# Another order of three ScalarE steps at four layer boundaries, and 17 matmuls of constants in two gaps of TensorE

## The chip, the core and the metric

The kernel runs on one core of a Trainium2 chip. The time is the device time of one execution in microseconds (us); lower is better. Engines are named as in the profile: PE is TensorE (PEld its weight load), ACT is ScalarE, DVE is VectorE, POOL is GpSimd, SP is SyncE, which issues the DMAs.

## What is computed

Two blocks on a sequence of 512 tokens of width 1024, in float32. The first has a convolution layer and an attention layer, each followed by a feed-forward layer, the second a gated delta rule beside sliding-window attention, and another feed-forward layer. Cut to what matters here:

```python
for layer in range(2):
    hn = rms_norm(h, mix_pre_g[layer])
    m = conformer_conv(hn, ...) if layer == 0 else mla_attention(hn, ...)
    h = h + rms_norm(m, mix_post_g[layer])
    f = squared_relu_mlp(rms_norm(h, ffn_pre_g[layer]), w_ff1[layer], w_ff2[layer])
    h = h + rms_norm(f, ffn_post_g[layer])
```

So after each of the four layers stands the same sequence: square the layer's output, sum it over the width, take the root, scale, add to the residual `h`, normalise again, and multiply by the next layer's weights. This is a boundary.

## The kernel before

Everything is held with the width on the partitions: 8 tiles of 128 by 512 tokens. All weights come as one stream of chunks of 128 x 2048 (1 MB), two buffers deep. A float32 product is made of three products of a high and a low part. For each chunk ACT copies the high part (`head`, L626, `whi<-wraw`), then POOL (L535) or, for the chunks at a boundary, DVE (`weights_low`, L1279) subtracts it from the raw weights to get the low part (`wlo`), and then PE multiplies: 48 matmuls of 512 columns for a chunk (L2113), or at a boundary 48 of 256 columns for each half of the tokens (L2136, `project_half`). `start_chunk` makes PE wait for the semaphore `lo_ready` of the chunk before its first matmul.

The order on every engine is written out by hand, and each engine works through its own list in that order. The four boundaries are called MIX0, FFN0, MIX1 and FFN1 after the layer that they end; they are the same code with other numbers. At boundary `i`, `last` is the last chunk of the layer. In a boundary the tokens are done in two halves (0 and 1), and the tiles in four pairs (m = 0 to 3):

- PE: chunks `last-1` and `last`, both for half 0, then both for half 1; then `last+1` half 0, `last+2` half 0, `last+1` half 1, `last+2` half 1. In the middle of `last+1` half 0, ahead of its tile k = 4, PE sums the squares of the last pair of half 1 (`post_sums(i, 1, (3, 4))`, L2150).
- DVE: empties the banks (`evac`), scales by the root (L1293), adds to the residual (L1299), takes the low part of the next operand (`low`, L1304), and in between makes `weights_low(last+1)` and `weights_low(last+2)`. The second stands behind `low` of tiles 4 to 7 of half 0, ahead of everything of half 1.
- ACT: squares (`post_square`, L668), roots (L673, L674), the high part of the next operand (`high`, L679), and `head` of the chunks.

At FFN0 two operands are made from one residual (`xh`/`xl`, then `hh`/`hl`); the second's eight low parts of half 0 stand on DVE right behind `weights_low(last+2)`.

The other two places are in the first layer. At the start of the kernel PE sums the squares of x with a matrix of ones (L2204) and then multiplies the first chunk (L2113), as soon as DVE has made the low part of the first tile of the normalised x (L1259). While it runs, ACT makes the diagonal tap weights of the convolution (L764), copies the high part of chunk 2 (L626) and then takes the sigmoid (L769) of chunk 0's result; DVE gates with it (L1416), and PE multiplies the first taps (`taps`, L2227). Behind the convolution PE sums the convolution's output and its squares (L2249, L2254), ACT and DVE take mean, root and SiLU and split the result tile by tile into `hh` and `hl` (L1514), and PE multiplies chunk "pw2" (`project(c0, hh, hl, need=operand("ln"))`), each tile as soon as its `hl` is there.

Of the kernel before, what the change touches and what calls it, by code (L numbers as in the profile page):

```python
# [24 lines left out]
P = 128  # L25
# [3 lines left out]
DT = D // P  # L29
# [110 lines left out]
def build(nc, A, out):  # L140
    ctx = ExitStack()
    with ctx:
        def sb(name, shape, dt=F32):
            return ctx.enter_context(nc.sbuf_tensor(name, shape, dt))

        def sem(name):
            return ctx.enter_context(nc.semaphore(name))
# [15 lines left out]
        K = sb("K", [P, N_CONST])  # L163
        PV = sb("PV", [P, N_VEC])
        small = sb("small", [P, N_COLS])
        ps = ctx.enter_context(nc.psum_tensor("ps", [P, 8, SEQ], F32))
# [15 lines left out]
        ident, ones, half_ones = map(const, ("ident", "ones", "half_ones"))  # L182
# [12 lines left out]
        pool_sum, TAP_BANK, ODD_BANK = (E[:, 0, :], E[:, 1, :]), (6, 7), (4, 5)  # L195
# [115 lines left out]
        pair_free = [sem("pair_free_even"), sem("pair_free_odd")]  # L311
# [72 lines left out]
        def weights(c):  # L384

            if c < DT and c // 2 % 2:
                return lent[c % 2][:, 0:CW], lent[c % 2][:, CW:2 * CW]
            return whi[:, c % 2, :], wlo[:, c % 2, :]

        def weights_free(eng, c, h=0):  # L390

            if c >= DT + 2:
                eng.wait_ge(chunk_done, h * 2 + (c - 1))
            elif c >= 4:
                eng.wait_ge(chunk_done, c - 3)

        def pair(c):
            return 2 * (c % 2)
# [5 lines left out]
        def emptied(eng, c, h=0):  # L404

            eng.wait_ge(pair_free[c % 2], h + (c // 2 + 1))
# [202 lines left out]
        def _(act):  # L609
            steps = [0]  # L610

            def step(ins):

                steps[0] += 1
                ins.then_inc(act_step, 1)
                act.wait_ge(act_step, steps[0])

            def head(c, h=0):

                if isinstance(h, int) and c + 2 * h >= N_CHUNK:  # L620
                    return
                p = c % 2
                w = WIDTH[c + 2 * h] if isinstance(h, int) else CW
                act.wait_ge(raw_loaded[p], h * 16 + 16 * (c // 2 + 1))
                weights_free(act, c, h)
                act.activation(weights(c)[0][:, 0:w], wraw[:, p, 0:w], ACT.Copy).then_inc(hi_ready, 1)  # L626
# [32 lines left out]
            def boundary(i):  # L659
                last = LAST[i]  # L660

                def post_square(m, half):
                    if half:
                        emptied(act, last - 3 + m)
                    else:
                        act.wait_ge(evac_half, 2 * i + m - 1)
                    s = 2 * (m - 2)
                    act.activation(sq_half[:, s:s + 2, :], Y[:, 2 * m:2 * m + 2, TOK[half]],  # L668
                                   ACT.Square).then_inc(post_sq, 1)

                def post_root_of(half):
                    act.wait_ge(post_summed, 2 * i + half + 1)
                    step(act.activation(POST[half], POST[half], ACT.Ln, scale=1.0 / D, bias=eps_rms))  # L673
                    act.activation(POST[half], POST[half], ACT.Exp, scale=-0.5).then_inc(post_root, 1)  # L674

                def high(s, j, half):
                    (name, at, hi, _), hi_sem, _, _ = pre_norms(i)[s]
                    act.wait_ge(resid_half, DT * i + DT // 2 * half + j // 2 + 1)
                    act.activation(hi[:, j, TOK[half]], resid[:, j, TOK[half]], ACT.Copy,  # L679
                                   scale=vec(name, at + j)).then_inc(hi_sem, 1)  # L680

                def pre_squares(half):
                    for m in range(DT // 2):
                        act.wait_ge(resid_half, DT * i + DT // 2 * half + m + 1)
                        act.activation(Z[:, 2 * m:2 * m + 2, TOK[half]], resid[:, 2 * m:2 * m + 2, TOK[half]],
                                       ACT.Square).then_inc(pre_sq, 1)

                for m in range(2):
                    c = last - 3 + m
                    head(c + 2)  # L690
                    emptied(act, c)
                    if m:
                        act.wait_ge(post_added, 3 * i + 1)
                    for n in range(2):
                        act.activation(SQ[:, n, :], Y[:, 2 * m + n, :], ACT.Square).then_inc(post_sq, 1)
                    if m == 0 and i == MIX0:
                        act.wait_ge(rel_summed, 1)
                        act.activation(rel_rows, ps[0:SW_H, 6, 0:RELW], ACT.Copy).then_inc(rel_copied, 1)
                act.wait_ge(post_added, 3 * i + 2)
                post_square(2, 0)  # L700
                post_square(3, 0)
                post_root_of(0)
                head(last + 1)
                post_square(2, 1)
                for j in range(6):
                    high(0, j, 0)
                head(last + 2)
                post_square(3, 1)
                for j in range(6, DT):
                    high(0, j, 0)  # L710
                post_root_of(1)
                if i == FFN0:
                    for j in range(DT):
                        high(1, j, 0)
                pre_squares(0)
                for j in range(DT):
                    high(0, j, 1)
                if i == FFN0:
                    for j in range(DT):
                        high(1, j, 1)  # L720
                    head(last + 3)
                pre_squares(1)
# [34 lines left out]
            c0 = START["pw1"]  # L757
# [72 lines left out]
            c0 = START["pw2"]  # L830
# [39 lines left out]
            c0 = START["latent"]  # L870
# [233 lines left out]
            for t in range(TT):  # L1104
                par = t % 2
                act.wait_ge(rows_summed, t + 1)
                c0 = COLS["state_decay"][0] + 8 * par
# [962 lines left out]
        def _(pe):  # L2070
# [19 lines left out]
            def project(c, hi, lo, h=0, k_tiles=DT, k0=0, need=None, second=None, second_need=None,  # L2090
                        paired=True, midway=None, hooks={}, start=True, bank=None):

                if start:
                    start_chunk(c, h)
                p = c % 2
                bank = 2 * p if bank is None else bank

                order = ([(n, k) for k in range(k_tiles) for n in range(2)] if need and paired else
                         [(n, k) for n in range(2) for k in range(k_tiles)])
                for n, k in order:  # L2100
                    if midway and (n, k) == (1, 0):
                        midway()
                    if (n, k) in hooks:
                        hooks[(n, k)]()
                    if n and second:
                        hi, lo = second
                    if need and n == 0:
                        need(k)
                    if second_need and n == 1:
                        second_need(k)  # L2110
                    w = slice(k * 2 * P + n * P, k * 2 * P + (n + 1) * P)
                    for q, (wt, xt) in enumerate(passes(hi, lo, *weights(c))):
                        ins = pe.matmul(ps[:, bank + n, :], wt[:, w], xt[:, k0 + k, :],  # L2113
                                        start=k == 0 and q == 0, stop=k == k_tiles - 1 and q == 2)
                    if isinstance(h, int) and c == N_CHUNK - 1 and (n, k) == (0, k_tiles - 1):
                        ins.then_inc(last_half, 1)
                ins.then_inc(chunk_done, 1)
# [64 lines left out]
            def operand(name):  # L2182
                return lambda k: pe.wait_ge(split_done, SPLIT0[name] + k + 1)

            def project_tokens(c, k_tiles, n_out, need=None, hooks={}):
# [13 lines left out]
                                            start=k == 0 and q == 0, stop=k == k_tiles - 1 and q == 2)  # L2199
                ins.then_inc(chunk_done, 1)  # L2200

            pe.wait_ge(ones_loaded, 16)
            pe.wait_ge(squares_added, 1)
            pe.matmul(ps[:, SUMS, :], ones, Y[:, 0, :], start=True, stop=True).then_inc(squares_summed, DT)  # L2204
            c0 = START["pw1"]
            ready = operand("mix0_pre")

# [57 lines left out]
            rest_sum(DT - 1).then_inc(rest_summed, 1)  # L2265
            rest_square(DT - 1)
            c0 = START["pw2"]
            project(c0, hh, hl, need=operand("ln"))

            def distance_bias():  # L2270
# [9 lines left out]
            def ffn(layer):  # L2280
# [11 lines left out]
                with pe.Fori(1, FF_BLOCKS - 1) as b:  # L2292
# [12 lines left out]
                    bank=LATENT_BANK)  # L2305
# [281 lines left out]
            for t in range(TT):  # L2587
# [40 lines left out]
                for lv in range(1, 6):  # L2628
# [4 lines left out]
                    for g in range(2):  # L2633
                        pe.wait_ge(level_x, 10 * t + 2 * lv + g - 1)
                        for i in range(2):
# [3 lines left out]
                                            start=True, stop=True)  # L2639
# [11 lines left out]
                    for g in range(2):  # L2651
# [3 lines left out]
                        for i in range(2):  # L2655
                            hp = slice((2 * g + i) * P, (2 * g + i + 1) * P)
                            ip, up = slice(i * P, (i + 1) * P), slice(HALF + i * P, HALF + (i + 1) * P)
                            if lv < 5:
                                ins = pe.matmul(ps[:, LEVEL_Q[g], ip], inverse[g][:, up], level_mask[:, hp],  # L2659
                                                start=True, stop=True)  # L2660
                            else:
                                ins = pe.matmul(ps[:, LEVEL_Q[g], up], level_mask[:, hp], inverse[g][:, up],
                                                start=True, stop=True)
# [201 lines left out]
```

## Time and profile before

| what | value |
|---|---|
| time, median of 3 runs | 1952.64 us (1952.09 to 1953.35) |
| profiled execution: its time | 1951.87 us |
| its span, first to last instruction | 1950.1 us |
| PE busy, share of the span | 1909.4 us, 98% |
| DVE busy | 824.0 us, 42% |
| ACT busy | 783.3 us, 40% |
| POOL busy | 681.5 us, 35% |
| mean granted clock of PE | 0.999 |

Between the span and the profiled execution's time lie 1.8 us. PE is busy nearly always, but the busy time counts matmuls whose ends are modelled and overlap, so where PE really waits is read from its waits and from the distances between matmuls.

### The profile page before, as it was taken

To read this page: it belongs to the slowest core of one execution; us is meant where nothing else is said; L and a number is where in the kernel's file an instruction comes from. 1 tells how busy PE (TensorE), PEld (TensorE's weight loads), DVE (VectorE), ACT (ScalarE), POOL (GpSimd) and SP (SyncE) were. 2 spreads that over 40 slices of the span, in tenths; PEclk is the share of its full clock that TensorE was granted. 3 is DMA by queue.
4 is the path that set the end of the run, shared out by engine and by line. 5 is a ranking of instruction groups with operands and counts; after the bars stand their busy time and mean duration, and the time that the engine had idled before them with its cause. 6 is when DMAs were issued, how large, how long until landed. Compare 5 with 4: busy or idle time off the path is not lost.

```text
span 1950.1 us, 24716 instructions
## 1 busy us (share of the span) xinstructions
PE 1909.4 (98%) x9804; PEld 1592.3 (82%) x9804; DVE 824.0 (42%) x1366; ACT 783.3 (40%) x1179; POOL 681.5 (35%) x217
## 2 busy tenths in 40 slices
PE   6998999999999999999999999999999999999999
PEld 4666988888897779888888897778898898888887
DVE  5996621111266474612111377756552352122122
ACT  6665432222345462523222256755454342122221
POOL 3993043434301210243343313222123403434442
PEclk9999999999999999999999999999999999999999
DMA  5211264222221211332322312111122322222322
GB/s 191 68 42 66 76 122 102 101 89 105 89 90 49 81 44 47 106 108 87 108 104 90 108 56 87 66 49 60 44 82 92 114 82 107 96 99 87 108 81 92
DMA packets 30510, 169.40 MB, mean 87 GB/s; under 512 B 3755, under 2 KB 6092, under 8 KB 13516
## 3 DMA queue, kind: packets, MB, share of 16 engines
q1 hardware_dynamic: 30412, 168.01, 25.8%
q8 instruction: 72, 1.18, 0.3%
q14 instruction: 26, 0.21, 0.0%
HBM read 162.22 MB, written 5.77 MB: 86 GB/s over the span
## 4 chain that ended last, share of the span: by engine, by line
PE 88%; DVE 5%; ACT 4%; POOL 2%; issue 1%; DMA 1%; SPq 0%; POOLq 0%; DVEq 0%; ACTq 0%
PE ps L2113 61%; PE ps L2136 8%; PE ps L2474 4%; PE ps L2541 3%; PE ps L2227 2%; POOL wlo L535 1%; PE ps L2638 1%; PE ps L2198 1%; ACT whi L626 1%; PE ps L2659 1%; DVE wlo L1279 1%; PE ps L2363 1%; PE ps L2380 1%; PE ps L2381 1%; PE ps L2398 1%
## 5 line engine op out<-in xcount | busy, mean ns | idle before, releaser
L535 POOL TENSOR_TENSOR wlo<-wraw,whi 128x2048 fp32r<-128x2048 f32 (+4 forms) x138 | 570.5, 4134 | 1192.1 <-ACT whi L626 1160.3
L626 ACT ACTIVATE whi<-wraw 128x2048 fp32r<-128x2048 f32 (+4 forms) x154 | 268.1, 1741 | 372.1 <-PE ps L2113 348.8
L2113 PE MATMUL ps<-xh,whi 128*128 128x512 f32 x980 | 386.7, 395 | 5.8 <-DVE xl L1259 4.3
L2113 PE MATMUL ps<-xl,whi 128*128 128x512 f32 x980 | 382.0, 390 | 0.0
L2113 PE MATMUL ps<-xh,wlo 128*128 128x512 f32 x980 | 381.9, 390 | 0.0
L2113 PE MATMUL ps<-hh,whi 128*128 128x512 f32 x752 | 295.3, 393 | 5.9 <-DVE hl L1514 5.7
L2113 PE MATMUL ps<-hh,wlo 128*128 128x512 f32 x752 | 293.1, 390 | 0.0
L2113 PE MATMUL ps<-hl,whi 128*128 128x512 f32 x752 | 293.1, 390 | 0.0
L2113 PEld LDWEIGHTS ps<-xh,whi 128*128 128x128 f32 x980 | 184.4, 188 | 48.3 <-issue 8.7
L2113 PEld LDWEIGHTS ps<-xl,whi 128*128 128x128 f32 x980 | 184.4, 188 | 39.3 <-issue 1.9
L2113 PEld LDWEIGHTS ps<-xh,wlo 128*128 128x128 f32 x980 | 184.3, 188 | 38.5
L2113 PEld LDWEIGHTS ps<-hh,whi 128*128 128x128 f32 x752 | 141.5, 188 | 37.7 <-issue 8.5
L2113 PEld LDWEIGHTS ps<-hl,whi 128*128 128x128 f32 x752 | 141.6, 188 | 30.0 <-issue 1.0
L2113 PEld LDWEIGHTS ps<-hh,wlo 128*128 128x128 f32 x752 | 141.4, 188 | 29.6
L848 ACT ACTIVATE hh<-Z 128x1024 fp32r<-128x1024 f32 x32 | 33.9, 1059 | 214.7 <-DVE Z L1560 212.0
L1560 DVE SCALAR_TENSOR_TENSOR Z<-ps,RS 128x1024 f32<-128x1024 f32 x28 | 34.3, 1224 | 183.2 <-PE ps L2113 183.2
L1437 DVE SCALAR_TENSOR_TENSOR ps<-Z,PV,ps 128x512 f32<-128x512 f32 x140 | 96.2, 751 | 8.4 <-ACT ps L801 4.1
L2136 PE MATMUL ps<-hh,whi 128*128 128x256 f32 x336 | 97.8, 291 | 0.0
L2136 PE MATMUL ps<-hh,wlo 128*128 128x256 f32 x336 | 95.1, 283 | 0.0
L2136 PE MATMUL ps<-hl,whi 128*128 128x256 f32 x336 | 95.0, 283 | 0.0
L2136 PE MATMUL ps<-xh,whi 128*128 128x256 f32 x304 | 88.1, 290 | 1.6 <-DVE xl L1304 1.6
L2136 PE MATMUL ps<-xl,whi 128*128 128x256 f32 x304 | 86.0, 283 | 0.0
(351 smaller groups left out, 2958.0 us busy)
## 6 DMA issues: line engine op xcount, KB each, us to landing
wraw<-stream SPq DMA_DIRECT2D x132, 1024.0 KB, 4.8
wraw<-stream SPq DMA_DIRECT2D x12, 768.0 KB, 4.1
wraw<-stream SPq DMA_DIRECT2D x6, 384.0 KB, 3.2
resid<-x SPq DMA_DIRECT2D x4, 512.0 KB, 5.1
wraw<-stream SPq DMA_DIRECT2D x8, 256.0 KB, 3.0
branch_scratch<-RS SPq DMA_DIRECT2D x8, 256.0 KB, 2.0
wraw<-stream SPq DMA_DIRECT2D x4, 512.0 KB, 3.7
rel_scratch<-E SPq DMA_DIRECT2D x8, 192.0 KB, 8.9
```

The source lines that it names most:

```text
L535: pool.tensor_tensor(lo[:, 0:w], wraw[:, p, 0:w], hi[:, 0:w], ALU.subtract).then_inc(lo_ready, 1)
L626: act.activation(weights(c)[0][:, 0:w], wraw[:, p, 0:w], ACT.Copy).then_inc(hi_ready, 1)
L848: act.activation(hh[:, 2 * j:2 * j + 2, :], t, ACT.Square)
L1279: dve.tensor_tensor(wlo[:, p, 0:w], wraw[:, p, 0:w], whi[:, p, 0:w], ALU.subtract).then_inc(lo_ready, 1)
L1437: dve.scalar_tensor_tensor(out=NT[:, at:at + 1, :] if last else acc, in0=x, scalar=tap(k, j, h), in1=acc, op0=ALU.mult, op1=ALU.add).then_ ...
L1560: ins = dve.scalar_tensor_tensor(out=t, in0=ps[:, 2 * p:2 * p + 2, :], scalar=0.0, in1=rs_pair(), op0=ALU.max, op1=ALU.mult)
L2113: ins = pe.matmul(ps[:, bank + n, :], wt[:, w], xt[:, k0 + k, :], start=k == 0 and q == 0, stop=k == k_tiles - 1 and q == 2)
L2136: ins = pe.matmul(half_bank(c, half)[:, n, :], wt[:, p, w], xt[:, k, TOK[half]], start=(n, k, q) == (0, 0, 0), stop=(n, k, q) == (1, DT - ...
L2198: ins = pe.matmul(dst, xt[:, k, t * P:(t + 1) * P], wt[:, p, k * n_out:(k + 1) * n_out], start=k == 0 and q == 0, stop=k == k_tiles - 1 an ...
L2227: ins = pe.matmul(ps[:, TAP_BANK[at], :], w, shifted(k, j, h), start=n == 0, stop=n == len(diags) - 1)
L2474: ins = pe.matmul(ps[:, slot_bank(s), :], wt[:, c % 2, w], xt[:, m // 3, :], start=m == 0, stop=m == 3 * DT - 1)
L2541: ins = pe.matmul(ps[:, bank, :], wt[:, p, w0 + k * P:w0 + (k + 1) * P], xt[:, k0 + k, :], start=r in (0, 24), stop=r == last)
```

## The change

There are three edits. At each of the four boundaries, ACT's `head(last + 2)` moves behind `post_square(3, 1)` and the two last high parts of half 0. At the start, PE multiplies constants six times behind the sum of the squares of x. Behind the convolution's sums it waits for the banks of the next chunk and multiplies constants eleven times, ahead of chunk "pw2". The results of these 17 multiplications are not used; each has 128 x 128 weights (the unit matrix) and 256 columns, in float32.

```diff
@@ boundary, ScalarE
                 post_square(2, 1)
                 for j in range(6):
                     high(0, j, 0)
-                head(last + 2)
                 post_square(3, 1)
                 for j in range(6, DT):
                     high(0, j, 0)
+                head(last + 2)
                 post_root_of(1)
@@ TensorE
+            def stay_awake(bank, times):
+
+                for n in range(times):
+                    pe.matmul(ps[:, bank, 0:2 * P], ident, K[:, 0:2 * P], start=True, stop=True)
+
             pe.wait_ge(ones_loaded, 16)
             pe.wait_ge(squares_added, 1)
             pe.matmul(ps[:, SUMS, :], ones, Y[:, 0, :], start=True, stop=True).then_inc(squares_summed, DT)
+            stay_awake(TAP_BANK[1], 6)
             c0 = START["pw1"]
@@ TensorE
             rest_square(DT - 1)
             c0 = START["pw2"]
+            pe.wait_ge(pair_free[0], DT // 2)
+            stay_awake(pair(c0), 11)
             project(c0, hh, hl, need=operand("ln"))
```

ACT's list at boundary MIX0, as a difference (minus is before, plus is after). `whi<-wraw` is the weights' high part, `SQ<-Y` the square of a pair, `xh<-resid` the high part of the next operand, the two rows on `ps` the root:

```order
 L668 ACTIVATE SQ<-Y 128x512 [waits pair_free_even]
 L679 ACTIVATE xh<-resid,PV 128x256 [waits resid_half] x6
-L626 ACTIVATE whi<-wraw 128x2048 [waits chunk_done,raw_loaded_odd]
 L668 ACTIVATE SQ<-Y 128x512 [waits pair_free_odd]
 L679 ACTIVATE xh<-resid,PV 128x256 [waits resid_half] x2
+L626 ACTIVATE whi<-wraw 128x2048 [waits chunk_done,raw_loaded_odd]
 L673 ACTIVATE ps<-ps,small 128x256 [waits post_summed]
 L674 ACTIVATE ps<-ps 128x256 [waits act_step]
```

The weights' high part now stands behind the square and two high parts that wait for a residual (`resid_half`). The lists of DVE, POOL and SP are the same as before, except that line numbers move.

PE's list between the convolution's sums (L2260 here, L2254 before) and chunk "pw2", in the changed kernel (before, the two rows of L2205 are not there, and the rest is the same):

```order
361 L2255 MATMUL ps<-Y,K 128x512 [waits conv_ready]
362 L2260 MATMUL ps<-SQ,K 128x512 [waits squares_ready]
363 L2205 MATMUL ps<-K 128x256 [waits pair_free_even]
364 L2205 MATMUL ps<-K 128x256 x10
365 L2113 MATMUL ps<-hh,whi 128x512 [waits split_done,pair_free_even,lo_ready]
366 L2113 MATMUL ps<-hl,whi 128x512
```

The first of the eleven waits for a semaphore for which the chunk's first matmul waits as well.

## Rows read from the trace of the kernel before

**Rows 1.** The page's chain of work that ended last, by engine.

```profile
PE 88%; DVE 5%; ACT 4%; POOL 2%; issue 1%; DMA 1%; SPq 0%; POOLq 0%; DVEq 0%; ACTq 0%
```

**Rows 2.** PE's waits: line, releaser, us in total, times, longest us.

```profile
PE ps L2113 <- DVE hl L1514: 5.7, 1, 5.7
PE ps L2113 <- DVE xl L1259: 4.3, 1, 4.3
PE ps L2150 <- ACT SQ L668: 2.6, 4, 0.8
...
PE ps L2136 <- DVE xl L1304: 1.6, 3, 0.6
```

**Rows 3.** Chain in order of time, one undisturbed chunk: start us, us, what.

```profile
68.00 10.92 PE ps L2113 x48
```

**Rows 4.** Stretches: us, busy (xcount) of PE, PEld, DVE, ACT, POOL; granted clock; DMA; GB/s.

```profile
18.20:21.60 3.40, 3.38 (x8) 2.72 (x9) 3.40 (x5) 0.94 (x2) 0.00 (x0) 1.00 0.26 100
...
165.30:168.30 3.00, 2.98 (x7) 2.42 (x8) 2.72 (x5) 2.32 (x4) 0.00 (x0) 0.50 0.00 0
```

**Rows 5.** Timeline of the kernel's start: start us, us, instruction, [idle before <- releaser].

```profile
11.85 2.05 PE L2204 MATMUL ps<-Y,K 128*128 128x512 f32 x2 [11.85 <-DVE Y L1391]
...
31.14 1.90 ACT L626 ACTIVATE hh<-wraw 128x2048 fp32r<-128x2048 f32 x1
...
32.94 0.66 ACT L769 ACTIVATE SQ<-ps,PV 128x512 f32<-128x512 f32 x1
...
34.53 3.67 PE L2227 MATMUL ps<-Z 128*128 128x512 f32 x8 [0.88 <-DVE Z L1416]
```

**Rows 6.** Timeline from the last taps to the second matmul chunk after "pw2" began.

```profile
136.86 8.82 PE L2227 MATMUL ps<-Z 128*128 128x512 f32 x20 [1.83 <-issue]
...
158.58 1.02 PE L2254 MATMUL ps<-SQ,K 128*128 128x512 f32 x2
...
165.32 0.77 PE L2113 MATMUL ps<-hh,whi 128*128 128x512 f32 x1 [5.72 <-DVE hl L1514]
...
167.84 0.69 DVE L1514 TENSOR_TENSOR hl<-ps,hh 128x512 fp32r<-128x512 f32 x1 [0.28 <-ACT hh L827]
...
174.69 0.69 DVE L1514 TENSOR_TENSOR hl<-ps,hh 128x512 fp32r<-128x512 f32 x1 [0.61 <-ACT hh L827]
...
177.70 0.39 PE L2113 MATMUL ps<-hh,whi 128*128 128x512 f32 x1
```

**Rows 7.** Timeline of ACT at boundary MIX1: weight copy of `last+2`, square, two high parts.

```profile
781.43 1.90 ACT L626 ACTIVATE whi<-wraw 128x2048 fp32r<-128x2048 f32 x1
783.24 0.61 ACT L668 ACTIVATE SQ<-Y 128x512 f32<-128x512 f32 x1
783.75 0.89 ACT L679 ACTIVATE xh<-resid,PV 128x256 fp32r<-128x256 f32 x2
```

**Rows 8.** Timeline of DVE and PE at boundary MIX1.

```profile
782.79 0.69 DVE L1299 TENSOR_TENSOR resid<-resid,Y 128x512 f32<-128x512 f32 x1
...
785.08 2.29 DVE L1279 TENSOR_TENSOR wlo<-wraw,whi 128x2048 fp32r<-128x2048 f32 x1
...
783.90 1.13 PE L2150 MATMUL ps<-SQ,K 128*128 128x256 f32 x4 [0.61 <-ACT SQ L668]
...
787.74 0.28 PE L2136 MATMUL ps<-xh,whi 128*128 128x256 f32 x1
```

**Rows 9.** Timeline of DVE and PE at boundary MIX0.

```profile
218.15 0.69 DVE L1299 TENSOR_TENSOR resid<-resid,Y 128x512 f32<-128x512 f32 x1
...
222.90 0.28 PE L2136 MATMUL ps<-xh,whi 128*128 128x256 f32 x1
```

**Rows 10.** Timeline of DVE and PE at boundary FFN0.

```profile
574.34 0.69 DVE L1299 TENSOR_TENSOR resid<-resid,Y 128x512 f32<-128x512 f32 x1
...
576.63 2.28 DVE L1279 TENSOR_TENSOR wlo<-wraw,whi 128x2048 fp32r<-128x2048 f32 x1
...
585.56 0.39 PE L2136 MATMUL ps<-xh,whi 128*128 128x256 f32 x1 [0.35 <-DVE xl L1304]
```

## Prediction

> **What bounds the kernel now.** I read the chain of work that ended last first: 88% of it is PE [rows 1], so a microsecond counts only if it takes a wait out of PE's list, speeds PE up, or puts a wait in. The next view is therefore the list of PE's waits [rows 2]. The four entries that the change touches are there. PE waits 5.7 us once for `hl` ahead of chunk "pw2", 4.3 us once for `xl` ahead of the first chunk, and 2.6 us in four places (0.8 at most) for ACT's square of the last pair, one at each boundary. The fourth, 1.6 us in three places, is PE waiting at FFN0 for the low parts of half 1 [rows 2, 10]; it is not meant by the change, but it tells that at FFN0 the second half runs at DVE's pace.
>
> The second thing to see is PE's rate. An undisturbed chunk takes 10.92 us for 48 matmuls of 512 columns, 0.2275 us each [rows 3]. Behind each of the two long waits it is half as fast: 7 matmuls in the 3.0 us from 165.3 on, 0.43 each, and 8 in 3.4 us from 18.2 on [rows 4]. 512 columns in 0.43 us is the 1.2 GHz level, against 2.4 GHz in the undisturbed chunk. The granted clock says 0.50 for the first stretch. For the stretch at the start it says 1.00, which the rate contradicts; I go by the rate. What PE did before was nothing, for 4.3 and 5.7 us. A pause of 1.83 us ahead of the last taps left it fast: the 20 records behind it took 0.44 us each [rows 6], the same as float32 records elsewhere in the convolution.
>
> **Six multiplications at the start: nothing.** They can save at most the slow rate, 8 times (0.425 - 0.2275) = 1.6 us of chunk 0. But who waits for chunk 0? ACT's sigmoid (L769) stands behind the copy of chunk 2's weights (L626), which runs from 31.14 to 33.04, and the sigmoid starts at 32.94, on its heels [rows 5]. Chunk 0 ends at about 18.2 + 3.4 + 40 x 0.2275 = 30.7 already. ACT's list up to there depends on DVE and the DMAs, not on PE's speed. DVE's gate and the taps at 34.53 hang on the sigmoid, and PE waits 0.88 us for them [rows 5]. A faster PE makes this wait longer, and the start of the taps stays. The cost is bounded the same way: twelve records of 256 columns (a float32 multiplication is two records), at the slow rate about 0.43 each, are 5.1 us from 13.6 on and end at 18.7, at most 0.5 us behind the 18.2 at which `xl` is there. That is less than the 0.88. So I take 0, with ends of 0 and -0.2.
>
> Here a rule of the Trainium skill is weighed. "TensorE: Matmul & The Clock Gate", Part 1, says that the throttled state is the default and that activity releases it. Read alone, it promises the 1.6 us; the trace agrees with the rule (slow behind both pauses) and yet gives it no time, since ACT's list sets the taps.
>
> **Eleven multiplications ahead of "pw2": -0.85 us.** They begin when the last sum is done, at 158.58 + 1.02 = 159.6 [rows 6]. A record of 512 columns takes 8.82/20 = 0.44 us [rows 6], one of 256 half of it; 22 records are 4.8 us and end at 164.4, 0.9 us before PE's next matmul at 165.32. Nothing is delayed, and a pause of 0.9 us is shorter than the 1.83 that left the rate high. Chunk "pw2" then runs fast from 165.32, but each tile must wait for its `hl`. Tile 2 has its own at 167.84 + 0.69 = 168.53, and from there on 6 matmuls a tile (1.37 us) never catch up with DVE: with 0.05 to hand over and 0.1 to restart, 168.69 + 36 x 0.2275 = 176.9. The last `hl` is there at 175.4, in time for tile 7 at 175.5. Before, the next chunk began at 177.70 [rows 6]. I take -0.85; the ends are 0 (the clock falls anyway) and -1.4 (all seven slow matmuls at full rate, 7 x 0.2).
>
> **The new order at the boundaries: +4.3 us.** The square no longer waits for the weight copy: at MIX1 it could start when the bank is emptied, over a microsecond before 783.24, and PE's 0.61 us there [rows 7, 8] would vanish. The four waits are 2.6 us together, plus a restart of 0.1 each (a first matmul behind a wait takes 0.39, others 0.28 [rows 8, 10]): 3.0 us, the upper end of the gain.
>
> But look at what moves back. `head(last+2)` now stands behind two high parts that wait for the residual of the last pair. At MIX1 DVE's add ends at 782.79 + 0.69 = 783.48 [rows 8]. From there it is a chain of single steps:
>
> - ACT hears of it 0.04 later (as PE of ACT's square: 783.85 to 783.90 [rows 7, 8]) and does the high parts; the next instruction starts 0.80 behind (0.89 less the overlap of 0.09 seen between ACT's rows [rows 7]): 784.32.
> - The weight copy takes 1.90: 786.22. DVE hears at 786.26.
> - `weights_low(last+2)` takes 2.29 [rows 8]: 788.55. Before, it started at 785.08, right behind `low` of tile 7, and was done at 787.37.
> - PE may start `last+2` half 0 at 788.60, and the restart adds 0.1: 788.71.
>
> Before, PE started it at 787.74 [rows 8], 0.4 us after the low part was there. Whatever PE wins at the square is lost while it stands ahead of this chunk, and 788.71 - 787.74 = 0.97 is lost besides. The chain from the end of the add to PE is 5.23 us long everywhere:
>
> - MIX0: add ends 218.84, PE at 224.07 instead of 222.90 [rows 9]: +1.17.
> - MIX1: +0.97. FFN1 is the same code with the same kinds of instructions: +0.97.
> - FFN0: here DVE's second half is the bound (PE waits for it at 585.56 [rows 10]), and all of it stands behind `weights_low(last+2)`. That would start at 575.03 + 0.04 + 0.80 + 1.90 + 0.04 = 577.81 instead of 576.63 [rows 10]: +1.18.
>
> Queued behind the copy on ACT is the root of half 1, behind the copy on DVE all of half 1: scaling, adding, low parts, each 1.2 us later. PE is itself 1.0 to 1.2 late there, and it waited for these low parts nowhere but at FFN0 [rows 2, 10], so I add nothing for them. The DMA into the freed raw buffer (issued by SP after `lo_ready`) is also 1.2 us later; its chunk isn't copied until the next layer's stream, and I add nothing. Sum: 1.17 + 1.18 + 0.97 + 0.97 = +4.3. The ends: if PE arrives as late as before (the square wins nothing) the chain is the same, so the lower end is an error of some 0.3 us per boundary in the handovers, +3; the upper end, half 1 late as well, +5.5.
>
> **Sum.** 0 - 0.85 + 4.3 = +3.45 us, on the profiled execution 1951.87 to 1955.3. The median of the runs is 0.77 above the profiled one, so I give 1952.64 + 3.45 = **1956.1 us**, 0.18% more. What a measurement of this kernel can tell from no change is about 0.2%, 3.9 us; the forecast lies just inside.
>
> **Rivals.**
>
> - *The move is only a gain.* The weight copy is hidden and the square's wait is gone. FFN0 gives nothing, DVE being its bound; 3 x 0.75 + 0.85 gives -3.1, 1949.5 us. For it speaks that the waits are real [rows 2]. Against it: PE has 0.4 us of slack ahead of `last+2` at MIX1 and the copy is 1.2 us later by single steps. It needs the low part to be there by some other way. Chance 0.07.
> - *The other side, slower: the constants don't hold the clock up.* Then "pw2" stays as it was and the sum is +4.3, 1956.9 us, 0.22%. It decides from a saving below 0.4 us. For it: nothing in the trace shows multiplications of constants, 256 columns wide. Against it: the float32 sums with a matrix of ones, just ahead in this stretch, are as plain, and their last two records still took 1.02 us with their modelled ends [rows 6], where two slow ones at the start took 2.05 [rows 5]. Chance 0.12.
> - *PE's clock falls in the new stalls.* PE would stand some 1.8 us ahead of `last+2` (the 0.75 won at the square and the 1.0 lost). If it fell each time, 7 matmuls' worth of slow running, 1.4 us, comes four times: +9, 1961.7 us. The 1.83 us pause that left the rate high speaks against it [rows 6]. Chance 0.03.
> - *The same mechanism, a size off.* Half 1's low parts late too, or handovers 0.15 longer: +4 to +5.5, 1956.6 to 1958.1 us. Chance 0.25.
>
> For the second of them the Trainium skill has a sentence that would bear on it: "TensorE: Matmul & The Clock Gate", Part 4, says that transposes (a multiplication with the unit matrix in the transpose mode) don't count as activity for the clock. The eleven use the unit matrix as weights; they are written as plain matmuls, not in that mode, so I leave the chance at 0.12. By that sentence, taken widely, the result would be the 1956.9 of the second rival.
>
> **How the numbers follow.** The forecast's own case, +2.5 to +3.9, has 0.53, and it is "same". The cases above +3.9 are the second rival, the third, and the size case: 0.40. The first gives 0.07 for faster. The range from 1953.0 to 1958.0 leaves out the gain, the fallen clock and the far ends.
>
> **What would show it.** In the changed trace PE's waits for the square are gone, and four waits of 1 to 1.8 us ahead of L2136 matmuls appear, released by DVE's `wlo` L1279. At MIX1 this instruction starts 2.7 to 2.8 us after the end of the add ahead of it, instead of 1.6. In "pw2" the first seven matmuls stand 0.23 apart, and the granted clock is 1.00. The taps at 34.53 don't move. The prediction is wrong if `wlo` is waited for nowhere, or if PE's slack ahead of `last+2` turns out larger than 0.4 us.

## The result and the profile after

The changed kernel takes 1955.39 us, the median of 20 executions (1954.75 to 1957.98); the kernel before, timed beside it 20 times, 1952.86 (1951.72 to 1954.46). The ratio is 1.0014, with a 95% interval of 1.0008 to 1.0021: 1.6 to 4.1 us longer, about 2.5. The interval leaves out no change, so the kernel is slower, by 0.14%. The forecast was 1956.1, range 1953.0 to 1958.0.

One thing must be known before the trace is read. The profiled execution of the changed kernel took 1957.98 us, the slowest of its twenty, with a span of 1956.2. Against the 1950.1 of before that is 6.1 us more, of which only a part is the change.

PE's list of waits in the changed kernel (line, releaser, us in total, times, longest us), to be held against [rows 2]:

```profile
...
PE ps L2136 <- DVE wlo L1279: 6.2, 4, 1.5
...
PE ps L2136 <- DVE xl L1304: 1.8, 3, 0.6
PE ps L2233 <- DVE Z L1416: 1.7, 2, 1.1
...
PE ps L2113 <- DVE hl L1514: 1.0, 1, 1.0
...
PE ps L2113 <- DVE xl L1259: 0.7, 1, 0.7
```

The square L668 is gone from the list. In its place stand four waits, 6.2 us in all, ahead of L2136 for DVE's low part of the weights, L1279. The two long gaps are filled: the 5.7 ahead of "pw2" became 1.0, and the 4.3 ahead of the first chunk is gone. The 0.7 for `xl` in the list is another wait, in the middle of that chunk (below). The waits for half 1's low parts (L1304) are 1.8 instead of 1.6, so half 1 is not held up further.

Timeline of boundary MIX1 (start us, us, instruction, idle before and releaser): ACT, then DVE, then PE, to be read against [rows 7, 8]:

```profile
786.19 0.63 ACT L668 ACTIVATE SQ<-Y 128x512 f32<-128x512 f32 x1 [0.48 <-DVE Y L1540]
787.70 0.91 ACT L679 ACTIVATE xh<-resid,PV 128x256 fp32r<-128x256 f32 x2 [0.88 <-DVE resid L1299]
788.51 1.90 ACT L626 ACTIVATE whi<-wraw 128x2048 fp32r<-128x2048 f32 x1
...
786.97 0.69 DVE L1299 TENSOR_TENSOR resid<-resid,Y 128x512 f32<-128x512 f32 x1
...
790.44 2.29 DVE L1279 TENSOR_TENSOR wlo<-wraw,whi 128x2048 fp32r<-128x2048 f32 x1 [1.20 <-ACT whi L626]
...
787.31 1.03 PE L2150 MATMUL ps<-SQ,K 128*128 128x256 f32 x4
...
792.79 0.39 PE L2136 MATMUL ps<-xh,whi 128*128 128x256 f32 x1 [1.54 <-DVE wlo L1279]
```

Read the brackets from the end. PE's sums of squares (L2150) have no wait any more. ACT's square is early, and then ACT stands idle for 0.88 us, until the residual is added at 787.66; only then come the two high parts and the weight copy. DVE finishes the low part at 792.73 and PE starts 0.06 later, 5.13 us after the end of the add. Before, the same distance was 4.26 [rows 8]; with the 0.1 that a first matmul behind a wait takes longer, the difference is the 0.97 of the table below.

Where the 6.1 us lie follows from fixed points in the two traces:

| stretch | before | after | difference |
|---|---|---|---|
| span's start to the taps | 34.53 | 35.32 | +0.79 |
| last 20 taps | 8.82 | 10.52 | +1.70 |
| "pw2", first matmul to the sums behind 54 | 13.90 | 13.21 | -0.69 |
| MIX0, FFN0, MIX1, FFN1 | | | +1.16 + 1.19 + 0.97 + 0.97 = +4.29 |

The first two are not the change. The start is the DMAs of this execution, not of the new code. Chain of the changed kernel, its first transfers (start us, us, what):

```profile
1.20 5.13 DMA resid<-x
7.19 7.23 DMA wraw<-stream
```

Before, the two took 4.70 and 6.86: 0.43 + 0.37 = 0.80 us less. Over the twelve traces of this study the taps begin anywhere between 33.79 and 35.79. The second is the clock. The taps in the changed kernel's timeline:

```profile
137.67 10.52 PE L2233 MATMUL ps<-Z 128*128 128x512 f32 x20 [1.83 <-issue]
```

And its windows there (columns as in [rows 4]):

```profile
137.00:138.00 1.00, 0.33 (x1) 0.36 (x2) 1.00 (x2) 0.40 (x1) 1.00 (x2) 0.91 0.00 0
...
139.00:140.00 1.00, 1.00 (x2) 0.34 (x1) 1.00 (x2) 1.00 (x2) 0.98 (x1) 0.50 0.06 16
140.00:141.00 1.00, 1.00 (x2) 0.34 (x1) 1.00 (x3) 0.85 (x3) 0.86 (x2) 0.50 0.00 0
141.00:142.00 1.00, 1.00 (x3) 0.46 (x2) 1.00 (x2) 0.98 (x3) 0.86 (x2) 0.89 0.00 0
142.00:143.00 1.00, 1.00 (x4) 0.50 (x3) 0.96 (x3) 0.99 (x2) 1.00 (x1) 1.00 0.03 8
```

Behind the same 1.83 us pause as in [rows 6] the granted clock fell to 0.50, the 1.2 GHz level, just after PE had resumed at 137.67 (0.91 in the first of these rows), and was back at 1.00 from about 141.2. In the other eleven traces it stayed at 1.00 here. The changed kernel's mean granted clock is 1.000 in 18 of its 20 executions and 0.999 in two, which took 1957.29 and 1957.98. Only the second of these has a trace; if the first is the same fall, two in twenty have it, and it hardly moves the median.

"pw2" in the changed kernel, its timeline:

```profile
161.95 4.91 PE L2205 MATMUL ps<-K 128*128 128x256 f32 x22
...
167.83 0.47 PE L2113 MATMUL ps<-hh,whi 128*128 128x512 f32 x1 [0.97 <-DVE hl L1514]
```

And its windows:

```profile
160.00:165.30 5.30, 5.30 (x21) 3.72 (x20) 2.92 (x5) 3.38 (x5) 2.85 (x3) 1.00 0.87 311
165.30:168.30 3.00, 2.03 (x10) 1.48 (x9) 2.16 (x5) 2.89 (x5) 2.11 (x2) 1.00 0.40 167
```

The constants take 4.91 us, end 0.97 before the operand is there, and the granted clock is 1.00 throughout. At the start they ran from 14.08 on:

```profile
14.08 4.87 PE L2205 MATMUL ps<-K 128*128 128x256 f32 x12
19.02 0.47 PE L2113 MATMUL ps<-xh,whi 128*128 128x512 f32 x1
...
22.70 0.50 PE L2113 MATMUL ps<-xh,whi 128*128 128x512 f32 x1 [0.68 <-DVE xl L1259]
...
33.73 0.66 ACT L769 ACTIVATE SQ<-ps,PV 128x512 f32<-128x512 f32 x1
...
35.32 1.10 PE L2233 MATMUL ps<-Z 128*128 128x512 f32 x2 [1.07 <-DVE Z L1416]
```

The taps start 1.59 us after ACT's sigmoid (L769), as they did before (32.94 to 34.53, [rows 5]); PE's wait for them grew from 0.88 to 1.07. The first chunk starts at 19.02 at full rate, but little of the gain gets as far as the taps: PE now catches up with DVE and waits 0.68 us at 22.70 for the low part of a later tile. From the first to the last of the 60 matmuls ahead of the taps it takes 33.86 - 19.02 = 14.84 us, where it took 33.27 - 18.22 = 15.05 before. These 0.2 us are what the wait for the taps grew by.

### The profile page after: what moved, and what is told of

The parts are those of the page before. It is cut to its first block, busy times and chain, and to the rows that moved or that the text cites. A ratio compares the mean times of both kernels' runs of the same rounds, so it can differ in the third digit from the quotient of the medians.

```text
span 1956.2 us, 24784 instructions
## 1 busy us (share of the span) xinstructions
PE 1919.3 (98%) x9838; PEld 1597.7 (82%) x9838; DVE 823.8 (42%) x1366; ACT 784.0 (40%) x1179; POOL 681.6 (35%) x217
## 3 DMA queue, kind: packets, MB, share of 16 engines
q8 instruction: 72, 1.18, 0.2%
## 4 chain that ended last, share of the span: by engine, by line
PE 87%; DVE 5%; ACT 4%; POOL 2%; issue 1%; DMA 1%; SPq 0%; POOLq 0%; DVEq 0%; ACTq 0%
PE ps L2113 61%; PE ps L2136 8%; PE ps L2482 4%; PE ps L2549 3%; PE ps L2233 2%; POOL wlo L535 1%; DVE wlo L1279 1%; PE ps L2646 1%; ACT whi L626 1%; PE ps L2198 1%; PE ps L2667 1%; PE ps L2371 1%; DVE Y L1293 1%; PE ps L2388 1%; PE ps L2389 1%
## 5 line engine op out<-in xcount | busy, mean ns | idle before, releaser
L2113 PEld LDWEIGHTS ps<-hl,whi 128*128 128x128 f32 x752 | 141.2, 188 | 29.7 <-issue 1.0
L2136 PE MATMUL ps<-hh,whi 128*128 128x256 f32 x336 | 97.8, 291 | 1.5 <-DVE wlo L1279 1.5
L2136 PE MATMUL ps<-hh,wlo 128*128 128x256 f32 x336 | 95.1, 283 | 0.0
L2136 PE MATMUL ps<-hl,whi 128*128 128x256 f32 x336 | 95.0, 283 | 0.0
L2136 PE MATMUL ps<-xh,whi 128*128 128x256 f32 x304 | 88.1, 290 | 6.5 <-DVE wlo L1279 4.6
L2136 PE MATMUL ps<-xl,whi 128*128 128x256 f32 x304 | 86.0, 283 | 0.0
```

Source lines behind the costliest of these rows:

```text
L2136: ins = pe.matmul(half_bank(c, half)[:, n, :], wt[:, p, w], xt[:, k, TOK[half]], start=(n, k, q) == (0, 0, 0), stop=(n, k, q) == (1, DT - ...
```

## The experiments

The theory: the boundary move costs 4.3 us, because the copy, the low part and `last+2` are one chain behind the last residual; the constants ahead of "pw2" give back a little; those at the start give nothing. The main rivals: the move is neutral and something else costs; or the square's place is what matters, not the copy's. Kernels of one group ran on one chip and share the executions of the kernel before: runs 1 to 4 are one group, 5 to 8 one, 9 and 10 one.

**1 to 3. Each edit alone, added to the kernel before.** The diffs are the three pieces of the change, one at a time.

The move alone: 

> The kernel before with only the new order on ScalarE at the four boundaries, without any multiplication of constants. Theory A (the weights' low part of chunk last+2 is late and TensorE waits for it): TensorE's waits for the square (2.6 us) are gone, four waits of about 1.5 us for wlo L1279 are there, and each boundary is 1.0 to 1.2 us longer, +4.3 us in all, 1957 us. Theory B (the move is a gain or costs nothing, and the 2.5 us that the changed kernel is slower come from the constants): no more than +1 us. The multiplications of the changed kernel bring 0.7 us in its trace, so A also asks that this kernel be 0.5 to 1 us above it.

The eleven constants ahead of "pw2" alone: 

> The kernel before with only the eleven multiplications of constants ahead of chunk pw2. If they hold the clock up: granted clock 1.00 from 165.3 on, chunk pw2 0.7 to 0.9 us shorter from its first matmul to the next chunk's, the median 0.7 to 0.9 us below before. If multiplications with the unit matrix don't count for the clock: the first seven matmuls 0.43 us apart as before, and no gain. If the pause's fast clock is worth more in most executions than in the profiled one of before: more than 1.2 us.

The six constants at the start alone: 

> The kernel before with only the six multiplications of constants at the start. Theory A: the first chunk's matmuls stand 0.23 us apart at once, TensorE's wait for DVE ahead of the first taps grows from 0.88 us to about 1.1, and the time stays within 0.3 us of before. Rival: the start is TensorE's after all, and up to 1.6 us are won.

| kernel | us | before | difference | ratio, 95% interval |
|---|---|---|---|---|
| move alone | 1956.52 | 1952.67 | +3.85 | 1.0010 to 1.0028 |
| "pw2" constants alone | 1950.82 | 1952.67 | -1.85 | 0.9982 to 1.0000 |
| start constants alone | 1952.28 | 1952.67 | -0.39 | 0.9988 to 1.0006 |

The three add up to +1.6, against the +2.5 of the whole; the intervals are some 1.8 us to either side, so they agree. At the boundaries the move alone has the waits of the changed kernel to the digit. PE's waits with the move alone:

```profile
PE ps L2136 <- DVE wlo L1279: 6.2, 4, 1.5
```

It carries the whole loss. The surprise is "pw2": -1.85 where the changed kernel's own trace showed 0.69. Its chain is as short as in the changed kernel (164.97 to 178.16, 13.19 us), so the difference must be in what it is compared with. With the start constants alone, "pw2" is unchanged code. Its chain has this row:

```profile
164.75 15.07 PE ps L2113 x54
```

And its windows for TensorE alone (PE's busy time, granted clock, DMA share, GB/s):

```profile
162.00:164.00 2.00, 0.00 (x0) 0.86 0.80 336
164.00:166.00 2.00, 1.25 (x3) 0.50 0.00 0
...
169.00:170.00 1.00, 1.00 (x3) 0.50 0.00 0
170.00:171.00 1.00, 1.00 (x5) 0.86 0.00 0
```

The clock fell while PE stood idle and came back only after 170, more than 5 us after PE had resumed, so that the stretch is 15.07 us long where [rows 6] gave 13.90 for it. At the start this kernel again shows the wait of 1.07 us ahead of the taps (and one of 0.62 inside the first chunk). Its timeline:

```profile
13.74 4.21 PE L2205 MATMUL ps<-K 128*128 128x256 f32 x12
...
33.92 2.38 PE L2233 MATMUL ps<-Z 128*128 128x512 f32 x5 [1.07 <-DVE Z L1416]
```

**4. The kernel before, unchanged, under another name.** 

> The kernel before itself, once more, for a second trace of it and for the noise of the comparison. The changed kernel's profiled execution lost 1.7 us in the last taps (granted clock 0.50 for 3 to 4 us behind the 1.83 us pause), which the profiled execution of before did not. If that is chance, this trace may show it or not, and the median is within 0.5 us of before. If the fall of the clock belongs to the changed kernel alone, neither this trace nor those of the three other kernels of this call that lack the start's constants show it.

1952.55 against 1952.67, interval 0.9988 to 1.0006: the scale on which the others are to be read. Its chain has

```profile
164.61 14.12 PE ps L2113 x54
```

The same code, and 0.22 longer than in the first trace. Over the seven traces without constants ahead of "pw2" this stretch took 13.90, 14.12, 14.39, 14.44, 14.88, 15.07 and 15.16, 14.57 in the mean; over the four with eleven it took 13.19, 13.19, 13.21 and 13.25. The gain is therefore 0.7 to 1.9 us by execution and 1.36 in the mean, and the one trace that I had before was the luckiest of seven.

**5. The square ahead of the copy, the high parts not.** It undoes half of the move:

```diff
                 for j in range(6):
                     high(0, j, 0)
+                post_square(3, 1)
                 head(last + 2)
-                post_square(3, 1)
                 for j in range(6, DT):
                     high(0, j, 0)
```

> The kernel before with the square of the last pair alone ahead of the weight copy; the two last high parts stay behind it, and no constants are multiplied. Theory A (what counts is when the copy starts, and so when DVE's low part of chunk last+2 is done): the copy starts about 1.1 us later than before, high part of tile 7 and with it wlo L1279 0.6 to 0.7 us later; TensorE's wait for the square is gone, waits of about 1 us for wlo are there, and the boundaries are longer by 0.4 (MIX1, FFN1), 0.55 (MIX0) and 0.6 us (FFN0): +2 us, half of what the whole move costs (+3.85 measured, +4.3 by its chain). Theory B (the cost is the two high parts ahead of the copy, and the square alone ahead of it is a gain): 0 to -3 us.

Measured: 1954.54 against 1952.43, +2.1 us, ratio 1.0010, 1.0001 to 1.0019. PE's waits:

```profile
PE ps L2136 <- DVE wlo L1279: 3.6, 4, 0.9
```

The square wait is gone here too, and still the kernel is slower, by about half as much. What counts is how late the copy starts, and each instruction ahead of it adds its own length and its own wait. That speaks against the rival on the square's place.

**6. Four constants instead of eleven ahead of "pw2".** Asks whether a shorter cover is enough: `stay_awake(pair(c0), 4)`, in the kernel before.

> The kernel before with four multiplications of constants ahead of chunk pw2 instead of eleven, so that TensorE pauses some 4 us between them and the chunk instead of 1. Theory: what holds the rate up is that TensorE's pause is short. Then after 4 us the clock is down or about to fall, the first matmuls are slow in some or all executions, and the median lies between before (0) and the eleven (-1.85): -0.3 to -1.5 us. Rival: any activity in the gap is enough: the rate is high as with eleven, and -1.2 to -1.9 us.

Measured: 1952.71 against 1952.43, ratio 1.0000, 0.9991 to 1.0009: no gain, where the theory had expected 0.3 to 1.5 us and its rival 1.2 to 1.9. The interval, 1.8 us to either side, hardly parts these; the trace does. Timeline of PE:

```profile
159.41 1.89 PE L2205 MATMUL ps<-K 128*128 128x256 f32 x8
165.29 0.47 PE L2113 MATMUL ps<-hh,whi 128*128 128x512 f32 x1 [3.99 <-DVE hl L1514]
...
167.06 0.73 PE L2113 MATMUL ps<-hh,whi 128*128 128x512 f32 x1
```

And the windows, with the columns as in run 3:

```profile
165.00:166.00 1.00, 0.71 (x3) 1.00 0.00 0
166.00:167.00 1.00, 1.00 (x4) 0.68 0.00 0
167.00:168.00 1.00, 1.00 (x3) 0.50 0.00 0
168.00:169.00 1.00, 1.00 (x4) 0.50 0.00 0
169.00:170.00 1.00, 1.00 (x5) 0.62 0.00 0
```

The pause left is 3.99 us. PE resumes at full speed at 165.29 (0.47 for the first matmul), and only about a microsecond later, with PE busy, the clock falls to 0.50 and stays there until about 170. The stretch takes 14.17 us, as long as without any constants.

**7 and 8. The copy early, and the low part of `last+2` moved from DVE to POOL.** If the chain behind the residual is what costs, the copy should stand ahead of more high parts, not behind them, and the low part needn't stand in DVE's list.

```diff
-BY_DVE = {c + i for c in LAST for i in range(3)} | ...
+BY_DVE = {c + i for c in LAST for i in range(3) if i < 2 or c == LAST[OUT]} | ...
...
-                for j in range(6):
+                for j in range(4):
                     high(0, j, 0)
                 head(last + 2)
                 post_square(3, 1)
-                for j in range(6, DT):
+                for j in range(4, DT):
...
-                weights_low(last + 2)
```

> A version that should keep the square's gain: no constants; at the four boundaries ScalarE copies the weights of chunk last+2 as soon as chunk last is done, ahead of the high parts of tiles 4 to 7 and of the square, and GpSimd, which is idle there, makes their low part instead of DVE. Theory A (the low part's arrival at TensorE is what the move made late): GpSimd's 4.6 us end at about the time at which TensorE, no longer waiting for the square, arrives; the boundaries MIX0, MIX1 and FFN1 are 0.5 to 0.6 us shorter than before, FFN0, where DVE is freed of 2.2 us, 1.7 to 2.2 us: -3.8 us, waits for the square and for xl at FFN0 gone or under 0.3 us. Rival: it is not the low part but something else behind the boundary (root, half 1) that sets the time: no more than -1 us.

With the eleven constants besides: 

> The version before this one with the eleven multiplications of constants ahead of chunk pw2. The two gains are in different places and should add up: -3.8 from the boundaries and -0.7 to -1.9 from chunk pw2, so -4.5 to -5.7 us, about 1947.5 us, below both kernels by more than the measurement's 0.2%. If the gains don't add, another wait has taken the place of one of them, and the trace names it.

Both missed widely: 1970.86 and 1970.45 against 1952.43, +18.4 and +18.0 us (ratios 1.0075 to 1.0102 and 1.0077 to 1.0108). The timeline of run 7 at MIX1, DVE and POOL:

```profile
787.77 0.69 DVE L1301 TENSOR_TENSOR resid<-resid,Y 128x512 f32<-128x512 f32 x1
...
790.67 4.83 DVE L1301 TENSOR_TENSOR resid<-resid,Y 128x512 f32<-128x512 f32 x1
...
790.43 4.52 POOL L535 TENSOR_TENSOR wlo<-wraw,whi 128x2048 fp32r<-128x2048 f32 x1 [31.93 <-ACT whi L628]
```

The same add, the same shape, takes 0.69 us alone and 4.83 when POOL's subtraction was issued 0.24 us before it. POOL ends at 794.95 and the add at 795.50, 0.55 later. That reads as an add that stood still until POOL was done and then ran its own length. PE's waits in run 7 show where most of the time went:

```profile
PE ps L2137 <- DVE xl L1306: 11.7, 3, 3.9
...
PE ps L2137 <- DVE hl L1306: 3.9, 1, 3.9
```

Four waits, 15.6 us, in place of the 4.2 for the square and for `xl` before [rows 2]. That is 11.4 of the 18.4 us. Much of the rest is the clock, which fell behind these waits. At MIX1 PE resumed at 795.95; its window (columns as in [rows 4]) and its chain:

```profile
795.00:801.00 6.00, 5.05 (x23) 5.05 (x24) 5.82 (x13) 5.14 (x12) 0.00 (x0) 0.50 0.50 175
...
795.95 16.99 PE ps L2137 x120
```

Before, the same 120 matmuls took 14.41 us. At the other three boundaries, too, the granted clock falls to 0.50 behind the wait.

Behind the rows of DVE and POOL the Trainium skill has a rule: "SBUF — State Buffer", section "Who interferes with whom", says that a VectorE instruction with two SBUF inputs and a GpSimd instruction that reads SBUF exclude each other, and the one issued later is blocked fully. The trace agrees, with its 0.69 and 4.83; at the other three boundaries the add beside POOL took 4.46 to 4.84.

**9 and 10. The copy early, everything on its own engine.** Only the order of ACT differs from before: `range(6)` becomes `range(4)` ahead of `head(last+2)`, and the other four high parts stand behind the square.

> No constants, all low parts on DVE as before, only ScalarE's order at the four boundaries: the copy of the weights of chunk last+2 goes ahead of the high parts of tiles 4 and 5 as well (it can start when chunk last is done), then the square, then the four high parts. So the square is ahead of TensorE and the copy isn't late. Theory A (the loss is wlo L1279's lateness): wlo starts when low of tile 7 is done, 0.2 to 0.3 us earlier than before; TensorE's waits for the square (2.6 us) are gone, waits of about 0.5 us for wlo are there instead, and each boundary is 0.1 to 0.3 us shorter: -0.4 to -1.0 us, no loss. Theory B (a square ahead of its old place, or anything else that the move did, costs time even with the copy in time): +1 us or more.

With the eleven constants besides: 

> The same with the eleven multiplications of constants ahead of chunk pw2, which alone took 1.85 us off the median (0.7 to 1.9 by the traces). If the two add: -2 to -2.8 us, about 1950.2 us, below both kernels. All of DVE's work stays off GpSimd's time, so no add of the residual takes over 0.7 us.

| kernel | us | before | difference | ratio, 95% interval |
|---|---|---|---|---|
| copy early | 1951.67 | 1952.21 | -0.54 | 0.9988 to 1.0006 |
| copy early, "pw2" constants | 1950.59 | 1952.21 | -1.62 | 0.9980 to 0.9998 |

PE's waits in run 9:

```profile
PE ps L2136 <- DVE wlo L1279: 1.0, 4, 0.3
```

And its chain at MIX1 and "pw2":

```profile
785.71 2.29 DVE wlo L1279
788.04 11.80 PE ps L2136 x96
...
165.03 15.16 PE ps L2113 x54
```

The four square waits (2.6 us) have turned into four of 1.0 us in all for the low part. That is the order that the move wanted, with the opposite sign of the edit: the copy goes ahead of two high parts instead of behind two. Its gain of half a microsecond can't be told from nothing. Run 10 has the lowest median of the study and lies below both kernels, by 1.62 us where 2.0 to 2.8 had been expected; nearly all of that is the constants, and it can't be told apart from run 2.

## Why the prediction held, and which term was off

Measured is +2.5 us with an interval of 1.6 to 4.1, forecast +3.45, its own case +2.5 to +3.9. So the result lies at the lower edge of that case, and the nearness of 1955.39 to 1956.1 owes 0.2 us to a kernel before that was itself timed at 1952.86 this time instead of 1952.64. The range's lower end, 1953.0, doesn't follow from the ends of the three terms, which add up to -0.2 - 1.4 + 3 = +1.4, or 1954.0; the result lies above either.

**The boundary move, +4.3: right in mechanism and size.** The trace has +4.29: 1.16, 1.19, 0.97 and 0.97, where 1.17, 1.18, 0.97 and 0.97 stood. `wlo` starts 790.44 - 787.66 = 2.78 us after the end of the add, foretold as 2.7 to 2.8. Alone it measured +3.85, and half of it (run 5) +2.1. The four new waits are 1.5 us, within the foretold 1 to 1.8. That PE gains nothing at the square showed as written: it reaches `last+2` earlier and waits there.

**Half 1 and the DMA at nothing: right.** L1304 has 1.8 us in three waits instead of 1.6.

**The start at nothing: right in size, and the reason only half of it.** -0.39 with an interval of 1.8 to either side; the taps follow the sigmoid by 1.59 us in both traces. But the prediction let the whole of the 1.6 us turn into a longer wait ahead of the taps, and that wait grew by only 0.19. Most of the gain was lost inside chunk 0, where the faster PE is held by DVE's low parts (0.68 us at one of them), a second limit that the prediction did not name. The cover is also thinner in some executions: in those of runs 7 to 9 PE did not wait ahead of the taps at all, and in that of run 9 the taps came 1.80 us behind the sigmoid instead of 1.59. There a faster chunk 0 might have given some 0.2 us; no measurement here resolves it. The sign "the taps at 34.53 don't move" was badly chosen, since their place differs by up to 2 us between executions of unchanged code. Their distance to the sigmoid was the sign.

**"pw2" at -0.85: the step that was mis-sized.** The mechanism held: clock 1.00, the second to the sixth matmul 0.23 apart, 13.21 us where I had worked out 13.05. But the term was the difference to one execution's 13.90, and over seven traces the unchanged stretch takes 14.57. The term is -1.36 in the mean of the traces, and -1.85 as measured alone. It is the traces that show this; the interval of run 2, 0 to -3.5 us, holds -0.85 too. With the traces' term the sum is +2.9, near the +2.5 measured; with mine it was +3.45.

**The rivals.** "Only a gain" is excluded by run 1. "The constants don't hold the clock up" is excluded by four traces with 1.00. "The clock falls in the new stalls" did not occur at the four boundaries of the changed kernel: the granted clock in its trace is 1.00 behind all four waits of about 1.5 us, and 18 of its 20 executions have a mean of 1.000. Behind the four waits of 3.9 us in run 7 it did fall. A fall behind a short pause did occur, at another place, the 1.83 us ahead of the last taps, which I had taken as proof that such a pause is safe. It is safe most of the time only.

**Still open.** Why the clock fell behind that pause in one trace of twelve and not in the others, and how long it stays down behind a long one, were not settled. Constants in the 1.83 us pause weren't tried: with so few executions that show a fall, worth 1.70 us, the median would not show them. That run 10 beats run 2 isn't shown.

## What to carry to other kernels

When an instruction is moved behind one that waits, write out the chain from what that one waits for to the next engine that needs the moved one's result; here it was add, high part, copy, low part, matmul, 5.1 us of single steps, and it priced the move within 0.1 us of what the trace shows. A stall that is taken out ahead of such a chain is worth nothing if the same engine waits for the chain's end.

A term whose size hangs on how long a slow clock lasts shouldn't be taken from one execution: look at the same stretch in several executions of unchanged code first. And before work goes from VectorE to an idle GpSimd, look at which two-input instructions of VectorE would be issued while it runs.

## What the runs showed of the hardware that was not expected

- The granted clock can fall after TensorE has resumed: behind a pause of 3.99 us it read 1.00 for about a microsecond of work and 0.50 for some 3 us after (run 6). Filling a third of a gap gained nothing; filling it up to the last microsecond held 1.00 in four traces.
- Behind each of four waits of 3.9 us the granted clock was 0.50, and at one of them 120 matmuls took 16.99 us instead of 14.41 (run 7). Behind the four waits of 1.5 us in the changed kernel it stayed at 1.00.
- Behind the same 5.72 us pause the slow stretch cost 0.7 to 1.9 us, by execution of the same code.
- Behind the same 1.83 us pause the clock fell in one of twelve traces, at a cost of 1.70 us.
- Plain float32 matmuls of the unit matrix, 256 columns wide, held the clock at 1.00 for 4.91 us. The Trainium skill, "TensorE: Matmul & The Clock Gate", Part 4, excludes transposes from what counts; these were not in the transpose mode, and the two don't contradict each other.
- VectorE's add of 128x512 took 4.83 us instead of 0.69 beside a GpSimd subtraction of 4.52 us, and ended 0.55 us behind it.
